# Chunk-pair output banks, panels fed with x before its norm, and a mask taken out of PSUM, in a two-block transformer kernel

## What is computed

```python
# block 1
h = rms_norm(x, norm1_w) * (1 + scale1) + shift1
gq, gk, gv, gz, ga, gb, sq, sk, sv = split(h @ w_in)
o_g = gated_delta_rule_chunked(q_g, k_g, v_g, g, beta)       # 8 heads of 64, chunks of 64 tokens
o_g = rms_norm(o_g, gdn_norm_w) * silu(heads(gz))
o_s = sliding_window_attention(q_s, k_s, v_s, sinks)         # 8 q heads, 2 kv heads, blocks of 128
x = x + gate1 * (concatenate([o_g, o_s]) @ w_out)
h2 = rms_norm(x, norm2_w) * (1 + scale2) + shift2            # norm 2
x = x + gate2 * ((silu(h2 @ w_gate) * (h2 @ w_up)) @ w_down) # width 2816
# one chunk of the delta rule
v_new = u_c - w_c @ S
o = qd_c @ S + qk_c @ v_new
S = S * dec_c + kd_c.T @ v_new
# block 2: 16 meta tokens ahead of x, 528 in all
h = rms_norm_2(h_res, pre_norm_g)                            # norm 3
cu = h @ w_in_2[...]; a, gate = split(cu); z = a * sigmoid(gate)   # conformer branch, then the others
```

## Time and profile before

| | us |
|---|---|
| median of three runs | 1363.29 (1363.13 to 1363.96) |
| profiled execution | 1363.27 |
| its span | 1361.5 |
| PE busy | 1288.0 (95%) |
| DVE busy | 676.7 (50%) |
| ACT busy | 476.4 (35%) |
| POOL busy | 117.0 (9%) |

### The profile page before, as it was taken

One profiled execution on the slowest core, in us unless ns is written; L12 is line 12 of the kernel. 1 busy time (PEld: TensorE's weight loads), 2 busy tenths in 40 slices (PEclk: granted clock), 3 DMA queues, 4 the chain that ended last, 5 costly groups with the idle time before them and its releaser, 6 DMA issues.

```text
span 1361.5 us, 20475 instructions
## 1 busy us (share of the span) xinstructions
PE 1288.0 (95%) x8688; PEld 1021.7 (75%) x8688; DVE 676.7 (50%) x1012; ACT 476.4 (35%) x798; POOL 117.0 (9%) x134
## 2 busy tenths in 40 slices
PE   3899998999998999999999989999899989999996
PEld 2577877889877888888888788987466657767775
DVE  5799878644535552333333358584834433223324
ACT  3534543653325222112232333125444532222232
POOL 4000006411010000000000100000112210000001
PEclk9899999999898999999999989999999999999998
DMA  8665610002021443233322423222301033333211
GB/s 291 214 218 177 198 63 34 3 3 65 1 93 62 155 144 95 78 116 120 97 58 78 147 63 94 85 76 58 90 0 51 1 102 102 94 81 81 81 62 62
DMA packets 141210, 125.77 MB, mean 92 GB/s; under 512 B 6728, under 2 KB 124769, under 8 KB 140992
## 3 DMA queue, kind: packets, MB, share of 16 engines
q1 hardware_dynamic: 137856, 119.62, 28.8%
q0 software_dynamic: 1520, 2.49, 0.6%
q10 hardware_dynamic: 1744, 2.36, 0.5%
HBM read 121.77 MB, written 2.10 MB: 91 GB/s over the span
## 4 chain that ended last, share of the span: by engine, by line
PE 85%; DVE 7%; ACT 3%; DMA 3%; issue 2%; POOL 1%; ACTq 0%; SPq 0%; DVEq 0%; POOLq 0%
PE bank L553 54%; PE bank L792 5%; PE bank L1088 5%; PE bank L646 5%; PE bank L1159 3%; PE bank L1116 2%; PE bank L1070 2%; PE bank L1042 2%; DMA arena<-in_meta_tokens_dram 1%; PE bank L741 1%; DVE wlo L1847 1%; DMA ring<-in_w_in_dram 1%; PE bank L764 1%; PE bank L1054 1%; PE bank L751 1%
## 5 line engine op out<-in xcount | busy, mean ns | idle before, releaser
L553 PE MATMUL bank<-hsplit,whi 128*128 128x512 f32 (+1 forms) x2032 | 602.6, 381 | 0.0
L553 PEld LDWEIGHTS bank<-hsplit,whi 128*128 128x128 f32 x2032 | 369.6, 188 | 85.1 <-issue 17.8
L553 PE MATMUL bank<-hsplit,wlo 128*128 128x512 f32 (+1 forms) x1016 | 380.1, 374 | 0.0
L1847 DVE TENSOR_TENSOR wlo<-ring,whi 128x2048 fp32r<-128x2048 f32 (+4 forms) x90 | 186.8, 2076 | 207.0 <-ACT whi L1355 206.7
L553 PEld LDWEIGHTS bank<-hsplit,wlo 128*128 128x128 f32 x1016 | 190.9, 188 | 34.8
L1355 ACT ACTIVATE whi<-ring 128x2048 fp32r<-128x2048 f32 (+4 forms) x90 | 156.2, 1737 | 102.3 <-DVE xT L2200 53.3
L553 PE MATMUL bank<-a_split,whi 128*128 128x512 f32 x308 | 94.8, 389 | 0.0
L2447 DVE TENSOR_TENSOR arena<-bank,tb 128x512 f32<-128x512 f32 x24 | 16.6, 692 | 126.0 <-PE bank L1088 106.2
L1088 PE MATMUL bank<-arena,ring 128*128 128x512 f32 x160 | 75.2, 602 | 1.3 <-DVE arena L2406 1.1
L1764 ACT ACTIVATE tb<-bank,V 128x512 f32<-128x512 f32 x30 | 20.5, 683 | 138.8 <-PE bank L553 138.7
L553 PEld LDWEIGHTS bank<-a_split,whi 128*128 128x128 f32 x308 | 57.8, 188 | 12.0
(11 more groups left out here) (401 smaller groups left out, 1688.3 us busy)
## 6 DMA issues: line engine op xcount, KB each, us to landing
ring<-in_w_ada_dram SPq DMA_DIRECT2D x24, 1024.0 KB, 5.2
ring<-in_w_in_dram SPq DMA_DIRECT2D x22, 1024.0 KB, 5.3
ring<-in_w_in_dram SPq DMA_DIRECT2D x34, 512.0 KB, 5.6
ring<-in_w_gate_dram SPq DMA_DIRECT2D x11, 1024.0 KB, 5.3
ring<-in_w_up_dram SPq DMA_DIRECT2D x11, 1024.0 KB, 5.4
ring<-in_w_down_dram SPq DMA_DIRECT2D x8, 768.0 KB, 4.8
ring<-in_w_down_dram SPq DMA_DIRECT2D x8, 640.0 KB, 4.5
ring<-in_w_out_dram SPq DMA_DIRECT2D x4, 1024.0 KB, 5.1
```

The source lines that it names most:

```text
L553: last = mm(o[0:m, 0:n], w[:, k, c0:c0 + m], rhs(s, k), start=k + i == 0, stop=k == kn - 1 and i == 2)
L1847: split_lo = splitter(dve, None, lambda lo, src, hi: tt(lo, src, hi, ALU.subtract))
```

## The change

- **Scores.** The keys are stored twice (rows 0 to 63 and 64 to 127, `kdup`) rather than padded. Each head's score is a matmul on 64 rows, and each has a bank of its own. POOL's memset is gone.
- **D mask.** DVE multiplies the tile out of PSUM and frees the bank; ACT's copy only signals `tA_moved`, and POOL's next mask waits for both.
- **Splits.** The splits of out0 and out1 stand earlier: ACT after the moves of sizes 16 and 32, DVE after the gathers c32 and c64. inv[0] lies in `tb[0]`.
- **Delta rule's end.** Output bank b holds chunks 2b and 2b+1 for all four j. It is filled at n = 2b+1; ACT squares and copies it; `out_lengths` sums its squares in a later step. The low parts of the mix 4 to 7 are made by DVE between the state copies.
- **Out projection.** Four tiles are open and take mix 4 to 7; the last length sum stands after the first of them, the head spreads (now transposes) after the second. Then tiles 0 and 1 take mix 0 to 3, then tiles 2 and 3. Tiles 4 to 7 follow by `project`.
- **Norm 2.** g0 takes x times its modulation (`raw_hi`, `raw_rest`, made after each residual), not yet divided by the root. `norm_stats` stands after chunk 1, `norm_spread` after chunk 3, and after chunk 5 `gate_shift`, the product of the shift with w_gate (`gate_acc`, eight DVE operations). The two tiles are multiplied by the spread factor on DVE (`gate_first_out`), and the Silu adds the bias. u0 takes the normalised h2 through `first_tiles`.
- **Norm 3.** The same for cug, with `conf_first_out`; cu opens its four tiles through `first_tiles`. The rope load waits for the last cgate tile.
- Some semaphores are merged (`act_vectors`, `dve_vectors`).

```diff
                 if u == 0:
-                    pe.wait_ge(*done("kpad"))
-                o = open_tile(pe, "ss", u)
+                    pe.wait_ge(*done("kdup"))
                 for p in range(2):
-                    last = mm(o[:, p * wk:(p + 1) * wk], sq[:, hp, b * WIN:(b + 1) * WIN],
-                              kpad[:, hp // 2, p, k0:k0 + wk], start=True, stop=True)
-                last.then_inc(*fill("ss", u))
+                    o = open_tile(pe, "ss", u, p)
+                    r = slice(p * HD, (p + 1) * HD)
+                    mm(o[:, 0:wk], sq[r, hp, b * WIN:(b + 1) * WIN], kdup[r, hp // 2, k0:k0 + wk],
+                       start=True, stop=True).then_inc(*fill("ss", u, p))
...
+            def out_at(j, n):
+                at = (n % 2) * NJ * CH + j * CH
+                return out_tile[n // 2][:, at:at + CH]
...
+            def out_lengths(b):
+                if b == 0:
+                    length_sum[0] = open_tile(pe, "osum", hold=True)
+                pe.wait_ge(*done("osq", b))
+                for j in range(NJ):
+                    c = 2 * (NB * j + b)
+                    last = mm(length_sum[0][:, c:c + 2], t2_all[:, j, b * P:(b + 1) * P], cst("two"), start=True, stop=True)
+                last.then_inc(*(fill("osum") if b == NB - 1 else signal("part")))
+
...
+                        last = product(out_at(j, n), gE[j], lambda n: q_of[j][:, n, :], (n,),
+                                       start=False, stop=n % 2 == 1 and j == NJ - 1)
+                    if n % 2:
+                        last.then_inc(*fill("go", n // 2))
+                        let_go("go", n // 2)
+                    if n % 2 and n > 1:
+                        out_lengths(n // 2 - 1)
...
+            def mix_step(m, k):
+                hi, lo = split_of(f"out{m // 2}")
+                c0 = P * (m % 2)
+                for i, (w, s) in enumerate(((hi, 0), (hi, 1), (lo, 0))):
+                    last = mm(mixed[m][:, :], w[:, k, c0:c0 + P], mix_of(s, k), start=k == 4 and i == 0, stop=k == 3 and i == 2)
+                if k == 3:
+                    last.then_inc(*fill("mo", m))
+                    last_tile_of[f"out{m // 2}"] = ("mo", m)
+                    let_go("mo", m)
+
+            pe.wait_ge(*done("w_lo", "out1"))
+            for k in (4, 5, 6, 7):
+                pe.wait_ge(*done("mix", k))
+                for m in range(4):
+                    mix_step(m, k)
+                if k == 4:
+                    out_lengths(NB - 1)
+                    let_go("osum")
+                if k == 5:
+                    for j in range(NJ):
+                        head_spread(j)
+            for pair in range(2):
+                for k in range(4):
+                    pe.wait_ge(*done("mix", k))
+                    for m in (2 * pair, 2 * pair + 1):
+                        mix_step(m, k)
+            for m in range(4, KD):
...
                         if i == 0 and name == "g":
-                            first_tiles("g0", h_ready("2"), [(("fg", c), P * c, T, hx) for c in range(2)])
+                            first_tiles("g0", lambda k: done("raw2", k), [(("fg", c), P * c, T, raw2) for c in range(2)],
+                                        between={1: [(norm_stats, "2")], 3: [(norm_spread, "2", diag)], 5: [(gate_shift,)]})
+                            continue
+                        if i == 0:
+                            first_tiles("u0", h_ready("2"), [(("fu", c), P * c, T, hx) for c in range(2)])
                             continue
                         for c in range(2):
...
+            def factor_out(tag):
+                act.wait_ge(*done("xn" + tag, KD - 1))
+                A(factor_of[tag], bank("spread" + tag)[:, :], ACT.Copy).then_inc(*read("spread" + tag))
+
+            def raw_hi(tag, k, weight):
+                A(raw_of(tag, 0, k), xT[:, k, :], ACT.Copy, scale=weight).then_inc(*signal("raw" + tag + "_hi", k))
...
+                if m in (1, 3, 5, 7):
...
             modulate("2", modA2, 24)
-            split_hi()
+            factor_out("2")
             for part, (c0, n) in enumerate(FFN_PARTS):
                 for i in range(c0 // 2, (c0 + n) // 2):
...
+                    split_hi()
             root("3", sroot, ("sum3",), 1.0 / D, epsc)
-            act.wait_ge(*filled("fu", KF - 1))
...
                         ins.then_inc(*signal("xn" + tag, k))
-                    if k == KD - 1:
-
-                        dve.wait_ge(*done("xn" + tag, KD - 1))
-                        v.engine_nop().then_inc(*read("spread" + tag))
+                    if k == KD + 1:
+                        dve.wait_ge(*copied("spread" + tag))
+                        first_out(factor_of[tag])
...
+            def raw_rest(tag, k, weight):
+                hi = raw_of(tag, 0, k)
+                dve.wait_ge(*done("raw" + tag + "_hi", k))
+                stt(out=raw_of(tag, 1, k), in0=xT[:, k, :], scalar=weight, in1=hi.bitcast(F32), op0=ALU.mult, op1=ALU.subtract)\
+                    .then_inc(*signal("raw" + tag, k))
...
-                    dve.wait_ge(*copied("tA", j - 1))
-                    tt(by_chunk(dd[j - 1][:, 0, :]), gA[j - 1], mask64("m16"), ALU.mult).then_inc(*signal("D", j - 1))
+                    dve.wait_ge(*done("tA_moved", j - 1))
+                    tt(by_chunk(dd[j - 1][:, 0, :]), whole("tA", j - 1), mask64("m16"), ALU.mult).then_inc(*read("tA", j - 1))
                 window(j)
             for j in range(NJ):
...
             for m in range(KD):
                 residual(("mo", m), m, 16)
+                raw_rest("2", m, modA2[:, m:m + 1])
                 if m in (1, 3, 5):
                     split_lo()
+                if m == 5:
+                    dve.wait_ge(*loaded("g0"))
+                    for k in range(KD):
+                        wk, shift = W("g0")[:, k, :], modT[:, 24 + k:25 + k]
+                        if k:
+                            dve.wait_ge(*done("gate_acc", k - 1))
+                            ins = stt(out=gate_acc, in0=wk, scalar=shift, in1=gate_acc, op0=ALU.mult, op1=ALU.add)
+                        else:
+                            ins = ts(gate_acc, wk, shift, None, ALU.mult)
+                        ins.then_inc(*signal("gate_acc", k))
...
+                dve.wait_ge(*filled("gshift"))
+                v.tensor_copy(gate_bias0, bank("gshift")[:, 0:2]).then_inc(*read("gshift"))
+                for k in range(2):
+                    dve.wait_ge(*filled("fg", k))
+                    last = tt(silug[k], bank("fg", k)[:, :], factor, ALU.mult)
+                    last.then_inc(*read("fg", k))
+
...
+            def conf_first_out(factor):
+
+                for m in range(2):
+                    for half in range(2):
+                        dve.wait_ge(*filled("cgate", m, half))
+                        o, at = bank("cgate", m, half), half * H2
+                        skip = 0 if half else META
+                        if skip:
+                            v.tensor_copy(conf_gate[m][:, 0:META], o[:, 0:META]).then_inc(*signal("part"))
+                        last = tt(conf_gate[m][:, at + skip:at + H2], o[:, skip:H2], factor[:, at + skip - META:at + H2 - META], ALU.mult)
+                        last.then_inc(*read("cgate", m, half))
+                    dve.wait_ge(*copied("cgate", m, 1))
+                    v.engine_nop().then_inc(*signal("cscaled", m))
+
```

293 lines of the change are left out of this document (156 added, 137 removed).

## The result

The changed kernel takes 1351.68 us (median of 4 executions, 1350.70 to 1352.49) against 1363.21 beside it: a ratio of 0.9915, 95% interval 0.9903 to 0.9927. It is 11.5 us faster where 22.3 were forecast, and just above the end of the range (1351.0).

What follows compares the result with a forecast made beforehand. PE was taken as the bound, busy 95% of the span (DVE 50%). Gains of 5.5 + 5.0 + 2.8 + 4.9 + 4.1 = 22.3 us took 1363.3 to 1341.0 us, with a range of 1330 to 1351.

Steps and rivals of the forecast that it cites:

- the clock's return: At the changed places PE would lose less time at half clock; the prediction counted on 9.7 us from it.
- part 1: Window attention's start and diagonal mask: memset gone, mask faster, PE idle shorter, clock not falling; 5.5 us gained (2.6 to 7).
- part 3: Delta rule's end and out projection: less PE work, less new waits and a clock drop; 2.8 us gained (1 to 6).
- part 4: Norm 2: g0 on raw x shortens the stretch to g1, with a new 2.3 us wait; 4.9 us gained (2.5 to 8).
- part 5: Norm 3: cug on raw x, but cu waits for cgate's banks; 4.1 us gained (3 to 10.6).
- Rival 3: Clock falls in three new thin stretches (transposes, statistics, length sums between tiles): +6 us, 1347; chance 0.10.
- part 2: Score tiles on two row halves: paired matmuls overlap, 0.42 us in each of 12 units; 5.0 us gained.
- Inverse: Delta rule's inverse: split halves placed earlier on ACT and DVE lie beside PE work of over 10 us; 0 charged.
- n=2: Delta rule's recurrence: state tile waits for the first output pair's bank, which ACT must square and copy; +1.4 us.
- out2: Out projection's third weight panel: its split is not ready after tiles 2 and 3, so PE waits +3.2 us.
- Rival 1: New waits at out2, g1 and cu's banks are not there: 1330; chance 0.22.
- The bounds: Sums of the terms' own limits over the whole kernel: 1354 with all low, 1325 with all high.

Runs made afterwards that it cites:

- e6: The changed kernel with useless matmuls on PE in six pauses, ahead of the waits: 1338.75 us, 10.0 us less than the control (e5).
- e5: The changed kernel run again unchanged, as the control in a second session: 1348.70 us, ratio 0.9896 to the kernel before.
- e7: The changed kernel with five waits taken away by reordering instructions and none filled: 1334.14 us, ratio 0.9792 to the kernel before.
- e8: e7 with useless matmuls in the three pauses left (window attention's second turn, norm 2's statistics, first MLA turn): 1328.33 us, ratio 0.9746 to the kernel before.
- e9: The kernel before the change with useless matmuls in ten places: 1353.82 us, ratio 0.9940 to the kernel before without them.

## Why the prediction was wrong

**The step that failed is the clock's return.** Without it the sum was 12.6 us, and 11.5 were measured. The prediction took 9.7 us from the clock, and 0.6 came: it charged the kernel before with its slow stretches at the places of the change (14.5 us) and the changed one with 0 (part 1), 1.1 (part 3), 1.5 (part 4) and 2.2 (part 5). Measured were 3.0, 3.1, 5.1 and 1.5, and 2.8 instead of 1.5 in a place that the change does not touch. That the clock could be had back, and that it is worth this much, e6 shows: 10.0 us for useless matmuls in six pauses. The rows it rested on showed half clock behind pauses, and from "shorter pause" it went to "no fall", for which there was no row. The trace of the kernel before even spoke against it: two of the three pauses that the prediction names, those at 345 and 403, ended with waits of only 1.1 and 1.4 us, ahead of matmuls of one or two columns, and the clock fell behind both (stretches at 347.5 and 405.5).

```profile
346.82 6.43 PE L911 MATMUL bank<-consts,arena 128*128 128x2 f32 x32 [1.14 <-DVE arena L2168]
...
404.92 0.38 PE L570 MATMUL bank<-consts,tb 128*128 128x1 f32 x2 [1.39 <-ACT tb L1589]
```

 Rival 3 had the mechanism, a fall in the new thin places, but priced it at 2 us for each of three, and had no short pauses among them. Of the three the statistics did lose the clock (3.4 us). The transposes kept it: the window of the changed kernel that holds the sixteen of head_spread is at 1.00.

```profile
350.30:352.10 1.80, 1.80 (x18) 1.00 0.00 0
```

By that, the rule of the Trainium skill that was cited there (TensorE: Matmul & The Clock Gate, PE-mode transpose) changed nothing here. Another section of the same page (Part 1: The HAM clock gate) says of the ramp at a kernel's start that it differs from run to run and costs under 1% of a typical kernel's span. That it differs agrees with e5 against the first profile (7.9 and 5.4 us ahead of 200 us). The 1% is not the measure here, as the clock falls again later: the stretches behind 200 us alone took 15.5 of 1349 us, 1.1%, more than the whole change moved.

Part by part, without the clock, the forecast first and the measured second:

- *Part 1*, 4.0 against 3.7, of which 0.4 belong to part 2. POOL's normalising came 3.1 us earlier (4.0 taken), and PE arrived 2.4 earlier instead of 1.1; so of its idle, which was to be under 2 us, 3.11 stayed. What PE itself gains ahead of a wait is lost in it; the prediction said so for 1.1 us, but left out that the four narrow score units get shorter too (0.2 each), which is worth nothing for the same reason.
- *Part 2*, 5.0 against 4.7 for eleven of its 12 units. Right, and the nearest row (L764 on column halves) was the right one to take.
- *Inverse*, 0 against -1.2: mis-sized at nothing. The cover named, PE work of over 10 us, hides ACT and DVE, but PE itself stood still in that work, in eight of the nine profiles with the earlier load; why is open.
- *Part 3*, -0.6 against -0.3 (its terms add up to 2.7, not 2.8), with the waits at n=2 (1.18 against 1.4) and ahead of out2 (2.96 against 3.2).
- *Part 4*, 2.2 against 3.0; *part 5*, 2.0 against 2.1.
- *MLA's start*: from the issue of its last DMAs to POOL's first product it is 13.1 us instead of 12.5, with the issue unchanged. In e5 it is 11.9, so 0.6 is within what executions differ by.
- *Rival 1* (the new waits are not there) was the one with 0.22, and no such wait was missing.

The range ended at 1351 and the time was 1351.7, with a control at 1348.7. The bounds gave 1354 (the other end, 1325, needs the 6.8 estimated for part 2; with 5.0 it is 1327); the range would have had to reach there, as the clock's part had no row for short pauses and its own bounds, from 0 to the whole 15, were not in the sum.

## What to carry to other kernels

An order of instructions can be followed to within 0.3 us of a wait (four of the five forecast; the fifth, the turn's, was 3.11 for "under 2"), but a wait's price is its length plus the slow stretch that may follow it (1.4 to 3.4 us here), and that stretch did not follow the wait's length. So count the pauses as well as adding them up, down to the 1.8 us of e7. A single profile in which the clock stays up behind a pause, or without one, proves little: look at the same place in several. Where a pause can't be taken away, useless matmuls ahead of the wait, a little shorter than it, keep the clock up (10 us here). In e8 and e9 the executions then also lay within 2.1 us of each other, in e6 they did not (5.0).
